# Layer 2 mixers: the last level of an inverse on one block, attention in two parts, another order at the seam

## The chip, the core and the metric

The kernel runs on one core of one Trainium2 chip. The metric is the device time of one launch in microseconds (us). Engines are named as in the profile: PE is TensorE (matmuls and transposes), DVE is VectorE, ACT is ScalarE, POOL is GpSimd, SP is SyncE, whose queue issues the DMAs. All data is float32.

## The reference, cut to what matters

The program is two layers on 1024 positions of 1024 features. Layer 2 projects its input, runs three mixers side by side (windowed attention with sinks, a state-space mixer called SSD, a gated delta rule called GDN), multiplies by an output matrix and ends with a feed-forward part. Only the mixers and what feeds them are touched.

```python
proj = h @ w_in
(a_q, a_k, a_v, s_z, s_xbc, s_dt, g_qkv, g_z, g_b, g_a) = jnp.split(proj, offs, axis=-1)
att = swa_sink_alibi(a_q, a_k, a_v, attn_sinks)          # 4 heads, scores over 3 chunks of 64
ssd = ssd_mixer(s_z, s_xbc, s_dt, ...)
gdn = gdn_mixer(g_qkv, g_z, g_b, g_a, ...)               # 4 heads
mix = jnp.concatenate([att, ssd, gdn], axis=-1) @ w_out

# in gdn_mixer, per head and chunk of 64:
strict = jnp.tril(kbeta @ k.T * decay, -1)
u, w = split(triangular_solve(I + strict, [v * beta, kbeta * exp(g)]))
v_new = u - w @ state
o = (q * exp(g)) @ state + (q @ k.T * decay) @ v_new
state = state * exp(g_last) + (k * exp(g_last - g)).T @ v_new
```

## The kernel before

**Stages.** Layer 1, then `layer2_projections` (24 units of 128 features: 14 through a convolution, 6 through a silu, 4 plain), `layer2_mixers`, the output product, and the feed-forward part, which takes the last third of the time. Each stage is a block at whose end the engines meet.

**Tiles.** `layer2_mixers` goes through 8 tiles of 128 positions (NT = 8). For GDN a tile is taken as one piece: its lower triangular matrix of 128x128 per head is inverted by doubling. A level b (2, 4, 8, 16, 32, 64) joins pairs of inverted blocks of b by b. With V the inverse so far (transposed) and VT its transpose, a level is

- `level_t(b)` on PE: the turn Y (V into VT, bank 7, copied by ACT), then T = NM_b x V for four heads into bank 5, where NM_b is the matrix times the mask of the level, made by POOL;
- a copy of T by ACT into T1 (`product(b)`), then `level_x(b)` on PE: X, the product of VT and T1, into bank 6;
- `level(b)` on DVE: V = V - X.

At level 64 the product goes into bank 7 instead and DVE corrects VT, which is what the chain reads next. T2, X2, Y2, V2 ... T64, X64, VT64 below are these steps. At level 64 only one block of a head isn't zero: 64 rows by 64 columns. Before, all of 128x128 is multiplied, copied and subtracted.

**Front and chain.** One round of the loop, `tile(n, i, t)`, works on the front of tile n (features turned, the scores of attention, SSD, the matrix of GDN) and on the chain of tile i = n - 1 (the six levels, then `wt`, `vn`, `o`, `ds`: the state's recurrence). The steps of both are written out in one order for each engine, and each engine takes its instructions in that order. The rounds: the front of tile 0 alone, seven rounds with front and chain (tiles 1 to 7 in front), and the chain of tile 7 alone. Signals are counters, one for each engine and each of front and chain (`Steps`): `done` raises it, `wait` waits for a step of the same tile, `wait_last` for that of the tile before.

**The steps named later**, with lines of the kernel before:

- PE: tr1 to tr4 and tr0 turn features into banks 1 to 4 and 0 (L2147); `ptr` turns the exponentials of attention, 8 pieces of 128x128 from `m_scores`; `yo` (m_ssd_state, m_bc); `v1t` turns VT0; `wt` (m_vt, m_kbg); `att` (m_v_prev or m_ga, with m_ptr); `vn` (m_gdn_state, m_wt and m_vbt, m_vt); `y` (m_xdt, m_sd); `o` (m_gdn_state, m_qgt and m_vn, m_qkd_chain); `ds` (m_vn, m_kd); `stn` (m_xde, m_vb). Matmuls are all recorded at L2151.
- DVE: `ysc` scales two sums of squares (L2018), V2 to V32 (L2012), VT64 (L2014), `xdt`, `xdec`, `yx` on SSD (L2088, L2090, L2100), `att` (L2104), `oss` (L2109), `og` (L2119), `y` (L2123), `yz` (L2125), `ogz` (L2130), `st2`, the new SSD state (L2134).
- ACT: two squares of Y with their sums (`yq0`, `yq1`, L1919), then `yln` and `yexp` on what ysc left, the copies of z and ga, VT2 (L1896) and T4 (L1899); four exponentials e0 to e3 (L1967), `es` (L1968), `pt`, the copy of the turned ones (L1971); the copy of `wt` (L1980).
- POOL: `nm0` to `nm5` (L1877), `kbg`, `kd`, `gzn` (L1849, waits for ogz of the tile before), `qgt`, `qkdc` and `bc` (copies, L47).

**Entry.** The projections write features to DRAM from ACT's results. The first 20 are read back for tile 0 while the last four are still being computed; these four (q, k and v of attention) are read back in `layer2_mixers` (L1818) when both stores have landed, and PE and POOL wait for `f_late`.

## Time and profile before

| | |
|---|---|
| three runs | 2499.05, 2503.95, 2503.97 us (median 2503.95) |
| profiled execution | 2499.8 us, its span 2498.0 us |
| PE, PEld, DVE, ACT, POOL busy in the span | 95%, 79%, 60%, 45%, 14% |
| granted PE clock, mean | 0.987 |
| layer-2 mixers | 1410 to 1733 us of the span |
| chain that ended last | 24% PE, nearly all in the feed-forward stage |

The page gives each engine's busy time over the whole span; the chain of waits on it covers only the end of the program, from 1848 us. The touched stage has to be read by itself, with windows and timelines.

### The profile page before, as it was taken

The numbers are of one execution on the slowest core, as the hardware profiler recorded it, in microseconds if no ns is written. First come the engines' busy times: TensorE is split into PE (matmuls) and PEld (weight loads), VectorE is DVE, ScalarE is ACT, GpSimd is POOL, SyncE is SP. The second block draws the span as 40 slices with busy tenths as digits, with TensorE's granted clock in tenths as the row PEclk, the third lists the DMA queues.
The fourth block names the chain that finished last, engine by engine and source line by source line (L and its number), as shares of the span: only waits on it lengthen the run. The fifth ranks groups of instructions, "written<-read, shape, count | busy, mean of one in ns | idle before, by whom it ended". The sixth has DMA issues, their size and how long they took to land. (4 is left out here: it accounts for less than half of the span.)

```text
span 2498.0 us, 33605 instructions
## 1 busy us (share of the span) xinstructions
PE 2369.3 (95%) x11568; PEld 1962.8 (79%) x11568; DVE 1506.1 (60%) x2096; ACT 1114.5 (45%) x1998; POOL 347.6 (14%) x361
## 2 busy tenths in 40 slices
PE   7999999999899999999999889987999999999997
PEld 6888888877778877787887778876877888888886
DVE  4657566665665546564551377775578677776556
ACT  4867677677443321242222255454333333323444
POOL 0423333333100000000000145442000000000000
PEclk9999999999999999999999899999999999999999
DMA  3111111110132264422223422211324434437764
GB/s 134 43 34 61 35 44 51 56 39 26 59 135 101 97 231 164 148 110 75 92 87 140 127 64 63 63 38 43 125 103 165 160 143 164 163 139 262 237 187 169
DMA packets 102886, 273.37 MB, mean 109 GB/s; under 512 B 9372, under 2 KB 35452, under 8 KB 98300
## 3 DMA queue, kind: packets, MB, share of 16 engines
q1 hardware_dynamic: 102780, 272.01, 31.5%
q8 instruction: 61, 1.00, 0.2%
q14 instruction: 45, 0.37, 0.1%
HBM read 196.16 MB, written 75.81 MB: 109 GB/s over the span
## 5 line engine op out<-in xcount | busy, mean ns | idle before, releaser
L52 PE MATMUL psG<-h_hi,w_hi 128*128 128x512 f32 x1056 | 262.6, 397 | 11.3 <-PEq L309 4.4
L52 PE MATMUL psG<-h_hi,w_lo 128*128 128x512 f32 x1056 | 257.8, 392 | 0.0
L52 PE MATMUL psG<-h_lo,w_hi 128*128 128x512 f32 x1056 | 257.5, 391 | 0.0
L52 PEld LDWEIGHTS psG<-h_hi,w_hi 128*128 128x128 f32 x1056 | 200.2, 192 | 55.4 <-issue 13.6
L82 DVE TENSOR_TENSOR w_lo<-w_raw,w_hi 128x1024 fp32r<-128x1024 f32 x82 | 104.8, 1280 | 223.5 <-ACT w_hi L77 223.1
L52 PEld LDWEIGHTS psG<-h_lo,w_hi 128*128 128x128 f32 x1056 | 198.6, 189 | 41.6
L52 PEld LDWEIGHTS psG<-h_hi,w_lo 128*128 128x128 f32 x1056 | 198.0, 188 | 41.3
L77 ACT CAST w_hi<-w_raw 128x1024 fp32r<-128x1024 f32 x84 | 88.0, 1048 | 146.7 <-PE psG L52 67.7
L366 POOL TENSOR_TENSOR sb_later_lo<-sb_later,sb_later_hi 128x512 fp32r<-128x512 f32 (+3 forms) x80 | 90.7, 1133 | 169.5 <-ACT sb_later_hi L395 169.5
L1831 POOL MEMSET m_k_prev<- 128x128 f32 x1 | 0.2, 204 | 770.1 <-POOLq L1517 770.1
L530 DVE SCALAR_TENSOR_TENSOR sb_sp<-psA,sb_tmp 128x128 f32<-128x128 f32 (+2 forms) x96 | 53.4, 556 | 73.5 <-ACT sb_tmp L384 72.8
L547 DVE TENSOR_TENSOR sb_w_lo<-sb_w,sb_w_hi 128x128 fp32r<-128x128 f32 (+2 forms) x96 | 64.0, 666 | 53.3 <-ACT sb_w_hi L402 52.1
L401 ACT ACTIVATE sb_w<-psA 128x128 f32<-128x128 f32 (+2 forms) x96 | 47.1, 491 | 86.6 <-PE psA L713 84.9
L363 POOL TENSOR_TENSOR sb_later<-sb_later,sb_sp 128x128 f32<-128x128 f32 (+2 forms) x64 | 70.5, 1102 | 27.5 <-DVE sb_sp L530 27.5
L1877 POOL TENSOR_TENSOR m_nm<-m_ntr,m_masks 128x512 f32<-128x512 f32 x48 | 64.5, 1373 | 68.8 <-DVE m_vt L2078 68.8
L47 POOL TENSOR_TENSOR sb_later<-sb_sp,sb_zero 128x128 f32<-128x128 f32 x56 | 42.1, 753 | 216.4 <-DVE sb_sp L534 216.4
L540 DVE TENSOR_TENSOR sb_sp_lo<-sb_sp,sb_sp_hi 128x128 fp32r<-128x128 f32 (+2 forms) x96 | 65.8, 685 | 0.0
L2674 DVE TENSOR_TENSOR h_ffn_lo<-ff_raw_up,h_ffn_hi 128x512 fp32r<-128x512 f32 x49 | 33.7, 690 | 43.9 <-ACT h_ffn_hi L2540 22.0
L2674 DVE TENSOR_TENSOR features_T<-ff_y,features_T 128x512 f32<-128x512 f32 x50 | 34.5, 690 | 39.9 <-PE ff_y L52 39.9
L2540 ACT CAST ff_a_hi<-features_T 128x512 fp32r<-128x512 f32 x40 | 24.6, 622 | 75.0 <-PE psH L52 34.6
L1620 DVE SCALAR_TENSOR_TENSOR p_acc<-p_raw,p_par,p_acc 128x1024 f32<-128x1024 f32 x42 | 54.0, 1285 | 5.5 <-DVE p_acc L1616 1.1
L2674 DVE TENSOR_TENSOR w_lo<-ff_raw_up,w_hi 128x512 fp32r<-128x512 f32 x39 | 27.0, 691 | 45.8 <-ACT w_hi L2632 45.8
(573 smaller groups left out, 5757.7 us busy)
## 6 DMA issues: line engine op xcount, KB each, us to landing
w_raw<-in_units SPq DMA_DIRECT2D x120, 512.0 KB, 4.1
w_raw<-hidden_blocks SPq DMA_DIRECT2D x77, 256.0 KB, 2.9
merge_gates<-features_T SPq DMA_DIRECT2D x12, 1024.0 KB, 7.3
merge_gates<-merge_gates SPq DMA_DIRECT2D x12, 1024.0 KB, 4.8
...
```

The source lines that it names most:

```text
L52: return pe.matmul(out, lhs, rhs, start=first, stop=last, skip_group_check=True)
L77: act.copy(self.hi[c % 2][:] if dest is None else dest, self.raw[c % 2][:]).then_inc(self.hi_done, 1)
L82: dve.tensor_tensor(self.lo[c % 2][:] if dest is None else dest, self.raw[c % 2][:], hi.bitcast(F32), ALU.subtract).then_inc(self.lo_done, 1)
L363: pool.tensor_tensor(later[:, q1:], later[:, q1:], sp_s[:, q1:], ALU.add).then_inc(later_ready, 1)
L366: pool.tensor_tensor(later_lo[(s + 1) % 2][:, q0:], later[:, q0:], later_hi[(s + 1) % 2][:, q0:].bitcast(F32), ALU.subtract).then_inc(late ...
L401: act.activation(w_t[:, first_query(s):], A[s % 3][:, first_query(s):], ACT.Exp).then_inc(exp2_done, 1)
L530: ins = dve.scalar_tensor_tensor(out[:, q0:], A[s % 3][:, q0:], 0.0, tmp[:, q0:], ALU.max, ALU.add)
L540: dve.tensor_tensor(sp_lo[s % 2][:, q0:], sp_t[s % 2][:, q0:], sp_hi[s % 2][:, q0:].bitcast(F32), ALU.subtract).then_inc(sp_lo_done, 1)
L547: dve.tensor_tensor(w_lo[s % 2][:, q0:], w_t[:, q0:], w_hi[s % 2][:, q0:].bitcast(F32), ALU.subtract).then_inc(w_lo_done, 1)
L1620: dve.scalar_tensor_tensor(acc[b][:], raw[b][:, t:t + T], par[:, bass.ds(n, 1), t], acc[b][:], ALU.mult, ALU.add).then_inc(step if t else ...
L1877: poolF.done(f"nm{m}", g.tensor_tensor(NM[:, m], NTR[:], over(MSK[:, 2 + m, :], GH), ALU.mult))
L2674: TT = lambda o, a, b, op: dve.tensor_tensor(o, a, b, op)
```

## The change

Five edits:

1. **Level 64.** T64, its copy, X64 and VT64 are cut to the block that isn't zero: T64 into partitions 64 to 127 and 64 columns per head, X64 into partitions 0 to 63 and 64 columns.
2. **Attention in two parts.** The turn of the exponentials waits for heads 0 and 1 and then for heads 2 and 3 (e1, e3) instead of for `es`. The products of attention for heads 0 and 1 stand ahead of `wt`, those of heads 2 and 3 behind it.
3. **DVE at the seam.** V2 comes first in a round, then `st2` of the tile before, then `ysc`.
4. **DVE at the end of a round.** `ogz` comes straight behind `og`, ahead of `y` and `yz`.
5. **Late features.** In the projections ACT writes the first 128 positions of each of the last four features from PSUM straight into tile 0's buffer, by one multiplication each ahead of the one it does anyway; the DMA at L1818 goes.

```diff
                             scale = 64 ** -0.5 if c < CONV + SILU + 2 else 1.0
+                            act.mul(D2.F[:, c, :], G[b][:, 0:P], scale).then_inc(D2.f_late, 1)
                             act.mul(res[b][:], G[b][:], scale).then_inc(silu_done[b], 1)
...
-                sp.dma_start(F[:, AQ0:, :], feats[AQ0:, :, 0:P].rearrange("c p t -> p c t")).then_inc(f_late, 16)
...
-                        scalG.done(f"T{b}", a.copy(T1[:].rearrange("p h t -> p (h t)"), bank(5)))
+                        if b < 64:
+                            scalG.done(f"T{b}", a.copy(T1[:].rearrange("p h t -> p (h t)"), bank(5)))
+                        else:
+                            scalG.done("T64", a.copy(T1[64:, :, 0:64], heads(PS[64:, 5, :], GH)[:, :, 0:64]))
...
-                            vectG.done("VT64", tt(flat(VT), flat(VT), bank(7), ALU.subtract))
-
+                            vectG.done("VT64", tt(VT[0:64, :, 64:], VT[0:64, :, 64:], heads(PS[0:64, 7, :], GH)[:, :, 64:], ALU.subtract))
+
+                    level(2)
                     if chain:
+                        vectF.wait(v, "st1", i)
+                        tensF.wait(v, "stn", i)
+                        vectF.done("st2", tt(ST[:], ST[:], bank(0), ALU.add))
                         scalG.wait(v, "yq1", i)
                         vectG.done("ysc", v.tensor_scalar(yss[:], yss[:], 1.0 / 256, EPS, ALU.mult, ALU.add))
-                    level(2)
...
                         for h in range(GH):
+                            if b == 64:
+                                x = mm(PS[64:, 5, h * P:h * P + 64], NM[:, LEVELS.index(b), h, 64:], V[:, h, 0:64])
+                                continue
                             x = mm(PS[:, 5, h * P:(h + 1) * P], NM[:, LEVELS.index(b), h], (V0 if b == 2 else V)[:, h])
...
-                                x = mm(PS[:, 7, h * P:(h + 1) * P], T1[:, h], vt[:, h])
+                                x = mm(PS[0:64, 7, h * P + 64:(h + 1) * P], T1[:, h, 0:64], vt[:, h, 64:])
...
-                        scalF.wait(pe, "es", n)
-                        turn(tensF, "ptr", 1, [SS[:, h, m * P:(m + 1) * P] for h in range(AH) for m in range(2)])
+                        for h in range(AH):
+                            if h % 2 == 0:
+                                scalF.wait(pe, f"e{h + 1}", n)
+                            for m in range(2):
+                                x = pe.transpose(PS[:, 1 + h // 2, (2 * (h % 2) + m) * P:(2 * (h % 2) + m + 1) * P], SS[:, h, m * P:(m + 1) * P], C["ident"][:])
+                        tensF.done("ptr", x)
...
                         turn(tensF, "v1t", 3, [VT0[:, h] for h in range(GH)])
+                        scalF.wait(pe, "pt", n)
+                        scalF.wait(pe, "ga", n)
+                        poolF.wait_last(pe, "vprev", n)
+                        attention(0)
```

`attention(first)` is the loop of before over two of the four heads. Not shown: the lines of `ogz` and `st2` at their old places, and that `f_late` is now waited for at 4 (one for each feature).

DVE at the seam from one round to the next, before (L1803 ends the loop's round; og, y, yz, ogz and st2 belong to the round that ends, ysc and V2 to the next):

```order
L2119 TENSOR_TENSOR m_og<-m_ps,m_orr 128x256 [waits m2_scalar_chain]
...
L2123 TENSOR_TENSOR m_y<-m_y,m_ps 128x512 [waits m2_vector_front]
...
L2125 TENSOR_TENSOR m_y<-m_y,m_z 128x512 [waits m2_vector_front]
...
L2130 TENSOR_TENSOR m_mix<-m_og,m_gzn 128x256 [waits m2_tensor_turned,m2_gpsimd_chain]
...
L2134 TENSOR_TENSOR m_ssd_state<-m_ssd_state,m_ps 128x512 [waits m2_tensor_front]
...
L2018 TENSOR_SCALAR m_yss<-m_yss 128x2 [waits m2_scalar_chain]
L2012 TENSOR_TENSOR m_v<-m_v,m_ps 128x512 [waits m2_scalar_front,m2_tensor_chain]
```

and after:

```order
L2125 TENSOR_TENSOR m_og<-m_ps,m_orr 128x256 [waits m2_scalar_chain]
...
L2129 TENSOR_TENSOR m_mix<-m_og,m_gzn 128x256 [waits m2_tensor_turned,m2_gpsimd_chain]
...
L2133 TENSOR_TENSOR m_y<-m_y,m_ps 128x512 [waits m2_vector_front]
...
L2135 TENSOR_TENSOR m_y<-m_y,m_z 128x512 [waits m2_vector_front]
...
L2015 TENSOR_TENSOR m_v<-m_v,m_ps 128x512 [waits m2_scalar_front,m2_tensor_chain]
L2023 TENSOR_TENSOR m_ssd_state<-m_ssd_state,m_ps 128x512 [waits m2_tensor_front,m2_vector_front]
L2025 TENSOR_SCALAR m_yss<-m_yss 128x2 [waits m2_scalar_chain]
```

ogz has moved up past y and yz, st2 has moved into the next round behind V2, and ysc (m_yss), which waits for ACT, stands behind both.

PE from the turn of the scores to wt, before (m_scores is ptr; m_v,m_nm is T64; m_vt,m_t is X64; c_ident,m_vt is v1t; m_kbg is wt):

```order
L2147 MATMUL m_ps<-c_ident,m_scores 128x128 [waits m2_scalar_front]
L2147 MATMUL m_ps<-c_ident,m_scores 128x128 x7
...
L2166 MATMUL m_ps<-c_ident,m_v 128x128 [waits m2_vector_chain]
L2166 MATMUL m_ps<-c_ident,m_v 128x128 x3
...
L2151 MATMUL m_ps<-m_v,m_nm 128x128 [waits m2_gpsimd_front]
L2151 MATMUL m_ps<-m_v,m_nm 128x128 x3
...
L2151 MATMUL m_ps<-m_vt,m_t 128x128 [waits m2_scalar_chain]
L2151 MATMUL m_ps<-m_vt,m_t 128x128 x3
...
L2147 MATMUL m_ps<-c_ident,m_vt 128x128 [waits m2_vector_front]
L2147 MATMUL m_ps<-c_ident,m_vt 128x128 x3
...
L2151 MATMUL m_ps<-m_vt,m_kbg 64x128 [waits m2_gpsimd_chain]
L2151 MATMUL m_ps<-m_vt,m_kbg 64x128 x3
```

and after:

```order
L2280 MATMUL m_ps<-c_ident,m_scores 128x128 [waits m2_scalar_front]
L2280 MATMUL m_ps<-c_ident,m_scores 128x128 x3
...
L2280 MATMUL m_ps<-c_ident,m_scores 128x128 [waits m2_scalar_front]
L2280 MATMUL m_ps<-c_ident,m_scores 128x128 x3
...
L2152 MATMUL m_ps<-m_v,m_nm 64x64 [waits m2_gpsimd_front]
L2152 MATMUL m_ps<-m_v,m_nm 64x64 x3
...
L2152 MATMUL m_ps<-m_vt,m_t 64x64 [waits m2_scalar_chain]
L2152 MATMUL m_ps<-m_vt,m_t 64x64 x3
...
L2148 MATMUL m_ps<-c_ident,m_vt 128x128 [waits m2_vector_front]
...
L2152 MATMUL m_ps<-m_v_prev,m_ptr 128x64 [waits m2_gpsimd_front]
...
L2152 MATMUL m_ps<-m_vt,m_kbg 64x128 [waits m2_gpsimd_chain]
L2152 MATMUL m_ps<-m_vt,m_kbg 64x128 x3
```

The turn waits twice, T64 and X64 have 64 partitions by 64 columns per head, and attention's first products (m_v_prev and m_ga, four in all) stand ahead of wt.

## Rows read from the trace of the kernel before

**Rows 1.** Windows: us, busy PE, PEld, DVE, ACT, POOL; PEclk, DMA, GB/s.

```profile
1415.00:1430.00 15.00, 11.78 (x61) 10.27 (x62) 11.31 (x15) 6.47 (x17) 3.24 (x4) 0.57 0.41 105
1547.63:1586.41 38.78, 35.06 (x280) 31.69 (x280) 27.29 (x47) 19.30 (x46) 17.32 (x20) 0.96 0.21 61
1661.34:1698.81 37.47, 33.44 (x281) 30.15 (x280) 27.23 (x47) 19.30 (x46) 17.28 (x20) 1.00 0.00 0
```

**Rows 2.** Timeline, PE, entry: start, us, engine line op, [idle before <-releaser].

```profile
1415.18 0.99 PE L2147 MATMUL m_ps<-c_ident,m_feat 128*128 128x128 f32 x7 [1.78 <-DMA m_feat<-features]
```

**Rows 3.** Timeline, ACT, entry.

```profile
1408.13 1.02 ACT L1572 ACTIVATE p_res<-psG 128x1024 f32<-128x1024 f32 x1 [9.85 <-PE psG L52]
```

**Rows 4.** Timeline, PE, back half of tile 4.

```profile
1572.82 1.09 PE L2147 MATMUL m_ps<-c_ident,m_scores 128*128 128x128 f32 x8 [0.64 <-ACT m_es L1968]
1573.75 0.60 PE L2166 MATMUL m_ps<-c_ident,m_v 128*128 128x128 f32 x4
1574.18 1.06 PE L2151 MATMUL m_ps<-m_v,m_nm 128*128 128x128 f32 x8
...
1576.06 1.16 PE L2151 MATMUL m_ps<-m_vt,m_t 128*128 128x128 f32 x8
1577.06 0.60 PE L2147 MATMUL m_ps<-c_ident,m_vt 128*128 128x128 f32 x4
1578.08 0.66 PE L2151 MATMUL m_ps<-m_vt,m_kbg 128*64 128x128 f32 x8 [0.42 <-DVE m_vt L2014]
...
1584.17 0.45 PE L2151 MATMUL m_ps<-m_vn,m_kd 128*64 128x64 f32 x8
```

**Rows 5.** Timeline, ACT, back half of tile 4.

```profile
1571.10 0.50 ACT L1967 ACTIVATE m_scores<-m_scores,m_ngm 128x256 f32<-128x256 f32 x1
...
1574.02 1.01 ACT L1971 COPY m_ptr<-m_ps 128x1024 f32<-128x1024 f32 x1 [1.25 <-PE m_ps L2147]
...
1575.41 0.60 ACT L1899 COPY m_t<-m_ps 128x512 f32<-128x512 f32 x1
...
1578.78 0.39 ACT L1980 ACTIVATE m_wt<-m_ps 128x256 f32<-128x256 f32 x1 [0.42 <-PE m_ps L2151]
```

**Rows 6.** Timeline, DVE, back half of tile 4.

```profile
1572.53 0.68 DVE L2012 TENSOR_TENSOR m_v<-m_v,m_ps 128x512 f32<-128x512 f32 x1
...
1577.26 0.69 DVE L2014 TENSOR_TENSOR m_vt<-m_vt,m_ps 128x512 f32<-128x512 f32 x1 [2.72 <-PE m_ps L2151]
...
1584.69 0.42 DVE L2109 TENSOR_REDUCE m_oss<-m_sqo 128x4 f32<-128x256 f32 x1 [1.45 <-ACT m_sqo L1984]
```

**Rows 7.** Timeline, PE, head of tile 5.

```profile
1588.40 1.15 PE L2151 MATMUL m_ps<-m_t,m_vt 128*128 128x128 f32 x8
...
1592.26 0.66 PE L2166 MATMUL m_ps<-c_ident,m_v 128*128 128x128 f32 x4 [1.94 <-DVE m_v L2012]
...
1594.55 1.16 PE L2151 MATMUL m_ps<-m_t,m_vt 128*128 128x128 f32 x8 [0.31 <-ACT m_t L1899]
```

**Rows 8.** Timeline, DVE, head of tile 5.

```profile
1587.83 1.04 DVE L2125 TENSOR_TENSOR m_y<-m_y,m_z 128x512 f32<-128x512 f32 x1
...
1589.13 0.67 DVE L2134 TENSOR_TENSOR m_ssd_state<-m_ssd_state,m_ps 128x512 f32<-128x512 f32 x1
1590.63 0.98 DVE L2018 TENSOR_SCALAR m_yss<-m_yss 128x2 f32<-128x2 f32 x1 [0.82 <-ACT m_sq L1919]
```

**Rows 9.** Timeline, POOL, head of tile 5.

```profile
1589.29 0.73 POOL L1849 TENSOR_TENSOR m_gzn<-m_ga,m_par_rows 128x256 f32<-128x256 f32 x1 [0.36 <-DVE m_mix L2130]
...
1590.55 1.04 POOL L47 TENSOR_TENSOR m_qkd_chain<-m_qkd,m_zero 128x512 f32<-128x512 f32 x1
...
1591.72 1.04 POOL L47 TENSOR_TENSOR m_bc<-m_feat,m_zero 128x512 f32<-128x512 f32 x1
```

**Rows 10.** Timeline, ACT, head of tile 5.

```profile
1593.91 0.59 ACT L1899 COPY m_t<-m_ps 128x512 f32<-128x512 f32 x1 [0.31 <-PE m_ps L2151]
```

**Rows 11.** Timeline, PE, last tile alone.

```profile
1703.15 0.66 PE L2166 MATMUL m_ps<-c_ident,m_v 128*128 128x128 f32 x4 [1.45 <-DVE m_v L2012]
```

More of the change, by code:

```diff
@@ L1793, in layer2_mixers @@
                                            "yo yx att st1 y yz st2")
-        vectG = Steps(sem("vector_chain"), "ysc V2 ym0 ym1 V4 V8 V16 V32 VT64 oss osc s0 s1 s2 s3 og ogz")
+        vectG = Steps(sem("vector_chain"), "V2 ysc ym0 ym1 V4 V8 V16 V32 VT64 oss osc s0 s1 s2 s3 og ogz")
         poolF = Steps(sem("gpsimd_front"), "par keep0 keep1 xd kprev nm0 nm1 nm2 vbt nm3 nm4 nm5 vprev")
@@ L1862, in tile @@
                         poolF.wait_last(g, "kprev", n)
-                        g.wait_ge(f_late, 16)
+                        g.wait_ge(f_late, PLAIN)
                         poolF.done("keep1", copy(g, AQK[:], F[:, AQ0:AQ0 + 3, :], zero))
@@ L2119, in tile @@
                         vectG.done("og", tt(heads(OG[:], GH), heads(PS[:, 6, 0:256], GH), per(orr[:], GH, 64), ALU.mult))
+                        vectG.wait(v, "og", i)
+                        poolG.wait(v, "gzn", i)
+                        tensH.wait_last(v, "mtrg", i)
+                        vectG.done("ogz", tt(M[:, 768:1024], OG[:], GZN[:], ALU.mult))
                     if front:
@@ L2125, in tile @@
                         vectF.done("yz", tt(Y[:], Y[:], Z[:], ALU.mult))
-                    if chain:
-                        vectG.wait(v, "og", i)
-                        poolG.wait(v, "gzn", i)
-                        tensH.wait_last(v, "mtrg", i)
-                        vectG.done("ogz", tt(M[:, 768:1024], OG[:], GZN[:], ALU.mult))
-                    if front:
-                        vectF.wait(v, "st1", n)
-                        tensF.wait(v, "stn", n)
-                        vectF.done("st2", tt(ST[:], ST[:], bank(0), ALU.add))
                 tiles(v, tile)
@@ L2286, in tile @@
                     if front:
-                        scalF.wait(pe, "pt", n)
-                        scalF.wait(pe, "ga", n)
-                        poolF.wait_last(pe, "vprev", n)
-                        for h in range(AH):
-                            kv = 64 * (h // 2)
-                            mm(PS[:, 1, 64 * h:64 * h + 64], PTR[:, 2 * h], VP[:, kv:kv + 64], True, False)
-                            x = mm(PS[:, 1, 64 * h:64 * h + 64], PTR[:, 2 * h + 1], GA[:, 256 + kv:320 + kv], False, True)
-                        tensF.done("att", x)
+                        tensF.done("att", attention(2))
                     if chain:
```

8 lines of the change are left out of this document (7 added, 1 removed).

## The prediction

> **What bounds the kernel now.** I read the windows view first, cut at the tiles of the layer-2 mixers, then the timelines of PE, ACT, DVE and POOL through one steady tile (tile 4 ends and tile 5 begins in it), then the entry and the tail. Only the mixer stage is touched: from 1410 to 1733 us of a span of 2498 us. The rest must keep its time, and the feed-forward stage behind it starts when the mixers end, so each us off this stage is a us off the whole.
>
> In the windows view the reader is to see that a steady tile takes 37.47 us and that PE is busy for 33.44 us of it, DVE for 27.23, ACT for 19.30, POOL for 17.28 [rows 1]. PE has the longest queue, but 4 us of idle time are left in it. The timelines show where: 1.94 us before Y2 (the turn after level 2), 0.31 before X4, 0.64 before the turn of the scores, 0.42 before wt [rows 4, 7]. So a tile goes at PE's pace except at four handovers, and both fewer PE instructions and shorter handovers count. There are seven periods from one T2 to the next, then a tail in which the last tile is alone.
>
> **Part 1, late features (once).** Before, PE waits 1.78 us for the DMA of the last four features [rows 2]. After, ACT writes them from PSUM, so the DMA and this wait go; nothing else holds PE there, as the three other turns are already done. Of the four new multiplications three lie beside PE's long products. The fourth stands ahead of the last big one, at 1408.13, for which the block's end waits [rows 3]. No row shows ACT on 128x128 from PSUM: between nothing and the 0.39 us of a 128x256 [rows 5]. I take 0.25. The DVE work behind this turn (the whole front of tile 0) shifts with it. Saved: 1.78 - 0.25 = 1.5 us; bounds 1.4 to 1.8, and less if another start-up step was just as late, which I put at 0.
>
> **Part 2, the back half of a tile (seven times).** Step by step, from the end of X32:
> - Turn of the scores. PE waits till 1572.82 for all exponentials. Exponential 1 runs at 1571.10 [rows 5], so it is done before X32 ends at 1572.18 - (0.64 of idle before 1572.82). Four of eight turns now go there; the other four wait for e3, which ends just before es, at about 1572.7, and take half of 0.93 (1572.82 to 1573.75). They end at 1573.2. Then Y32 wants V32, which ends at 1572.53 + 0.68 = 1573.21 [rows 6]. Y32 starts at about 1573.26 instead of 1573.75: 0.49 saved. With a later e3 it is 0.3; it can't be more, V32 is next.
> - T64 becomes 64 weight columns by 64 moving columns, four times. The trace has this form: ds, four matmuls in 0.45 us, where T64 takes 1.06 [rows 4]; less the overlap of about 0.1 us at their ends, 0.5 us saved. Bounds: nothing, if a fixed cost per matmul and not its size sets the pace, and 0.6. I take the row of the same form.
> - X64 waits for ACT's copy of T64 as well as for PE. ACT: the copy of the turned scores starts as their second half ends, 0.63 earlier than 1574.02 (1573.39), so the T64 copy starts at 1574.78 instead of 1575.41, and on 64x256 takes at most the 0.39 us of the 128x256 [rows 5]. It ends at 1575.16; PE is free at 1576.06 - 0.49 - 0.5 = 1575.07. X64 starts at 1575.2 instead of 1576.06, 0.86 saved, with ACT the later by 0.1.
> - X64 has the form of ds too: 0.38 us till the next instruction instead of 1.00 (1576.06 to 1577.06). 0.62 saved.
> - The turn behind it (v1t) to wt took 1.02 us (1577.06 to 1578.08), of which four turns are 0.47 and the rest is the wait for VT64. Now half of the attention stands in between, and VT64 is ready: before, it started 1.20 after X64 [rows 4, 6]; now at 1575.2 + 1.20 - 0.62 = 1575.8, and on 64x256 it takes at most the 0.42 of oss, so it ends at 1576.2, 1.75 earlier. The wait goes: 0.55 saved. What is late next: the copy of wt on ACT, hidden behind the other half of the attention.
> In sum 0.49 + 0.5 - 0.1 + 0.62 + 0.55 = 2.0 us, after which PE's queue is full up to the next T2. Its cover on DVE: DVE idled 1.45 us before oss [rows 6]; oss moves up by 2.0, the work from VT64 on by 1.75, so 1.2 us of cover is left. Seven times 2.0 = 14.0 us.
>
> **Part 3, the seam (seven times).** Before, V2 on DVE stood behind ysc, which waits for ACT's squares and ends at 1591.61; X2 was done at 1589.55 [rows 7, 8]. Now V2 starts at 1589.6 and Y2 follows the turns that end at 1592.26 - 1.94 = 1590.32. So Y2 and T4 come 1.9 us earlier. But X4 does not, as ACT must first do ysc's followers (ln, exp), the copies of z and ga and VT2, and only then T4. What X4 gains is (a) the 0.31 us that ACT waited for T4 [rows 10], and (b) whatever ysc gains. ysc stands behind st2 now and can start at 1589.6 + 0.6 + 0.6 = 1590.8, 0.2 later than before. Its end, though, was set elsewhere: it took 0.98 us for two numbers and ended 0.02 us after POOL's qkdc (1590.55 + 1.04) [rows 8, 9]. qkdc comes 0.36 us earlier, as ogz goes ahead of y and POOL no longer waits for it at gzn [rows 9]. So (b) is 0.36. X4: 0.67 us earlier, seven times 4.7 us. Bounds: -0.5 (below) to 1.0 us a tile, if ysc found DVE free of POOL. ogz ahead of y makes yz end 0.34 later, at 1589.2; the squares that read it start at 1589.7 and V2 at 1589.6, so it costs nothing. st2 after V2 ends before PE's next use of the state and of bank 0.
>
> By the Trainium skill (SBUF — State Buffer, "Who interferes with whom") DVE and GpSimd share a pair of ports, and a DVE instruction with two inputs in SBUF, or a tensor_scalar in a two-port mode, is held for a whole GpSimd instruction. The trace agrees at ysc and at yz (1.04 us, where st2 on the same shape, with one input in PSUM, takes 0.67) [rows 8]. By that rule ogz and yz, moved under kbg and kd, may be held by up to 0.6 us each, which the slack of 0.5 us nearly hides.
>
> **Part 4, the tail (once).** V2 no longer stands behind ysc: of 1.45 us of idle time before Y2 [rows 11] 0.5 goes. T64's and X64's forms and VT64 give 0.6 + 0.7 + 0.3, with nothing beside them. 2.1 us.
>
> **Sum.** 1.5 + 14.0 + 4.7 + 2.1 = 22.3 us. The profiled execution took 2499.8 us, the three runs 2499.05, 2503.97, 2503.95: the same program is found at two levels 4 to 5 us apart, so the sum is taken from between, 2501.9. That gives 2479.6; from 2499.8 it would be 2477.5, from 2503.95 2481.7. One term is left out: in tile 4 the granted clock was 0.96 and the tile took 38.78 us, 1.3 more than its sisters [rows 1]; such a dip may go or another come.
>
> **Rivals.**
> - Held ports (0.18). ysc now starts 0.2 us later. If it misses the end of qkdc it ends with bc, 1592.76 - 0.36 = 1592.4 [rows 9], 0.8 later than before; less 0.31 that is a loss of 0.5 a tile instead of a gain of 0.67, 8 us in seven. For it: both moved edges are within 0.4 us. Against: the same instruction got through at qkdc's end in the tile shown. The same mechanism could use up the 1.2 us of cover before oss (yx and xdec have two inputs in SBUF; a POOL instruction on 128x512 is 1.04 us, and two of them are more than 1.2). 2488.
> - Narrow products no cheaper (0.08). T64 and X64 keep 0.9 and 1.0 us because writing or reading a half of the partitions costs the same. Then 1.1 us a tile and in the tail goes: 22.3 - 8.9 = 13.4, 2488.5. Against it: ds, the same form.
> - PE slower (0.04), the one that ends on the other side. The granted clock is at half for most of tile 0 (0.57 from 1415 to 1430 us) [rows 1], where PE had idled and waited; the change leaves PE idle in one piece of 1.5 us before X4, with narrower work around it. A dip costs 1.3 us [rows 1], so 17 dips in seven tiles, two or three in each, eat the gain; three in each make 2507. Against: the four idle pieces of a tile fall from 3.3 us to about 1.9 in sum, and before had one dip in seven periods.
> - More than forecast (0.10): tile 0 goes at full clock, or ysc runs free: 2472 to 2474.
> - That PE waits as before because the order is not what it says is excluded by the instruction order.
>
> **Numbers.** Forecast 0.60, with its own range 2475 to 2485. Over all cases: 2472 to 2491. A change within 0.2% (5 us, about what can be told from none) needs nearly all of part 2 to fail: 0.02. Slower by more than that 0.03, faster 0.95.
>
> **What would show it.** The period from T2 to T2 at 34.8 us instead of 37.47; T64 and X64 at about 0.45 us each; no idle time before wt; before Y2 less than 0.1 us of idle time and 1.4 us before X4, ended by ACT; ysc ending with qkdc; oss still waiting for ACT; no DMA wait at 1413 us. Wrong would be: an idle PE before y or o (DVE late), ysc ending with bc, a granted clock under 0.97 from tile 1 on.

## The result, and the profile after

The kernel after takes 2487.93 us (median of 6 runs, 2484.43 to 2491.8), the kernel before 2503.81 us beside it (6 runs, 2499.05 to 2505.5). The ratio is 0.9940, interval 0.9928 to 0.9952: 16 us faster, where 22.3 were forecast. The time lies 8 us above the likeliest number, 2479.6; 2 of them come from the kernel before, which took 2503.8 and not the 2501.9 that the sum started from. The profiled execution took 2485.86 us, its span 2484.1 us.

| us, from the starts of PE's rows | before | after | gained | forecast |
|---|---|---|---|---|
| first turn of the mixers to T2 of tile 1's round | 25.06 | 22.32 | 2.7 | 1.5 |
| seven periods from T2 to T2 | 263.14 | 251.41 | 11.7 | 18.7 |
| last T2 to the first output product | 36.62 | 35.45 | 1.2 | 2.1 |
| the mixers | 324.82 | 309.18 | 15.6 | 22.3 |

So the shortfall lies in the periods. (The first row starts behind the new multiplications, whose 0.18 us is not in it.) Window of a steady tile after (columns as in [rows 1]):

```profile
1579.42:1615.17 35.75, 32.98 (x281) 29.41 (x280) 29.03 (x47) 19.09 (x47) 17.88 (x20) 1.00 0.23 66
```

A tile takes 35.74 us, not 34.8. PE has only 0.5 us less to do than in [rows 1], and DVE, whose VT64 now takes 0.41 us and not 0.69, is busy for 1.8 us more. That is the first trace of the cause.

PE, back half of a tile, against [rows 4]:

```profile
1566.45 1.36 PE L2280 MATMUL m_ps<-c_ident,m_scores 128*128 128x128 f32 x8
1567.69 0.66 PE L2167 MATMUL m_ps<-c_ident,m_v 128*128 128x128 f32 x4
1568.28 0.68 PE L2152 MATMUL m_ps<-m_v,m_nm 128*64 128x64 f32 x8
1568.89 1.13 PE L2152 MATMUL m_ps<-m_ssd_state,m_bc 128*128 128x256 f32 x4
1569.95 0.68 PE L2152 MATMUL m_ps<-m_vt,m_t 128*64 128x64 f32 x8
1570.56 0.66 PE L2148 MATMUL m_ps<-c_ident,m_vt 128*128 128x128 f32 x4
...
1571.98 0.66 PE L2152 MATMUL m_ps<-m_vt,m_kbg 128*64 128x128 f32 x8
```

Its weight loads (PEld) at three places where the width of the weights changes (128*64 stands for 64 weight columns):

```profile
1568.28 0.54 PEld L2152 LDWEIGHTS m_ps<-m_v,m_nm 128*64 128x64 f32 x8 [0.17 <-issue]
...
1569.95 0.54 PEld L2152 LDWEIGHTS m_ps<-m_vt,m_t 128*64 128x64 f32 x8 [0.33 <-ACT m_t L1902]
...
1572.57 0.30 PEld L2152 LDWEIGHTS m_ps<-m_v_prev,m_ptr 128*128 128x128 f32 x2 [0.17 <-issue]
```

T64 and X64 take 0.68 us, not 0.45; there is no idle time before wt. Before T64, and behind wt, PEld stands still for 0.17 us with nothing to wait for; behind T64 and behind X64, where the width changes as well, it is 0.07 us. Before X64 it waits 0.33 us for ACT's copy of T64.

PE at the head of the next round, against [rows 7]:

```profile
1584.02 0.66 PE L2167 MATMUL m_ps<-c_ident,m_v 128*128 128x128 f32 x4 [0.70 <-DVE m_v L2015]
...
1587.27 1.16 PE L2152 MATMUL m_ps<-m_t,m_vt 128*128 128x128 f32 x8 [1.26 <-ACT m_t L1900]
```

DVE from the back half to the head, against [rows 6, 8]:

```profile
1572.20 1.22 DVE L2094 TENSOR_TENSOR m_xdt<-m_xs,m_par 128x512 f32<-128x512 f32 x1
...
1575.17 1.08 DVE L2106 TENSOR_TENSOR m_y<-m_y,m_xd 128x512 f32<-128x512 f32 x1
...
1576.52 1.42 DVE L2111 TENSOR_TENSOR m_ssd_state<-m_ssd_state,m_par 128x512 f32<-128x512 f32 x1
1577.86 0.40 DVE L2115 TENSOR_REDUCE m_oss<-m_sqo 128x4 f32<-128x256 f32 x1
1578.30 0.79 DVE L2117 TENSOR_SCALAR m_oss<-m_oss 128x4 f32<-128x4 f32 x1
...
1580.86 0.65 DVE L2129 TENSOR_TENSOR m_mix<-m_og,m_gzn 128x256 f32<-128x256 f32 x1 [0.19 <-DVE m_og L2125]
1581.43 0.67 DVE L2133 TENSOR_TENSOR m_y<-m_y,m_ps 128x512 f32<-128x512 f32 x1
1582.14 1.23 DVE L2135 TENSOR_TENSOR m_y<-m_y,m_z 128x512 f32<-128x512 f32 x1
1583.29 0.67 DVE L2015 TENSOR_TENSOR m_v<-m_v,m_ps 128x512 f32<-128x512 f32 x1
...
1584.49 0.38 DVE L2025 TENSOR_SCALAR m_yss<-m_yss 128x2 f32<-128x2 f32 x1
```

DVE has no idle time before oss any more: xdt, yx and the decay of the SSD state (L2111) take 1.08 to 1.42 us beside POOL, where they took 0.69, 0.69 and 0.80. ogz takes 0.65 us and starts 0.19 after og, whose result it reads; yz ends 3.95 us behind T2 (before: 2.46), and V2 starts straight behind it.

One short instruction matters for what follows: `osc`, which scales the four sums of oss (L2117). In every period of all fourteen kernels og starts 1.15 to 1.16 us behind its end, and it ends itself 0.02 to 0.03 us behind an nm of POOL. Before, it took 0.48 us; first DVE, then POOL, before and after:

```profile
1585.15 0.48 DVE L2111 TENSOR_SCALAR m_oss<-m_oss 128x4 f32<-128x4 f32 x1
```

```profile
1582.66 4.17 POOL L1877 TENSOR_TENSOR m_nm<-m_ntr,m_masks 128x512 f32<-128x512 f32 x3
```

```profile
1575.67 4.63 POOL L1877 TENSOR_TENSOR m_nm<-m_ntr,m_masks 128x512 f32<-128x512 f32 x3
```

The three nm start 3.75 us ahead of T2 in both. After, they take 0.46 us more, all of it in the second one (1.71 us, before 1.27), beside the decay, which now stands under it. osc ends 0.03 us behind that second nm after, 0.02 before; so it ends 0.45 later against T2, and og with it. In the last tile, where POOL makes no nm, osc takes 0.17 us in every kernel.

ACT and POOL beside it, against [rows 10] and [rows 9]:

```profile
1583.40 0.42 ACT L1922 ACTIVATE m_sq<-m_y 128x256 f32<-128x256 f32 x1 [0.59 <-DVE m_y L2135]
```

```profile
1582.09 0.73 POOL L1849 TENSOR_TENSOR m_gzn<-m_ga,m_par_rows 128x256 f32<-128x256 f32 x1
1582.78 1.06 POOL L47 TENSOR_TENSOR m_qgt<-m_qt,m_zero 128x256 f32<-128x256 f32 x1
1583.80 1.03 POOL L47 TENSOR_TENSOR m_qkd_chain<-m_qkd,m_zero 128x512 f32<-128x512 f32 x1
```

The squares now wait 0.59 us for yz. ysc ends 0.04 us after qkdc (before: 0.02). POOL no longer waits at gzn, as forecast, but qgt takes 1.06 us where it took 0.61, beside yz, and ends 0.47 us behind yz's end.

The entry, PE and ACT, and the tail, against [rows 2, 3, 11]:

```profile
1412.91 3.80 PE L2148 MATMUL m_ps<-c_ident,m_feat 128*128 128x128 f32 x19 [2.68 <-DVEq L1726]
```

```profile
1410.26 0.28 ACT L1572 ACTIVATE m_feat<-psG 128x128 f32<-128x128 f32 x1 [9.69 <-PE psG L52]
```

```profile
1691.22 0.66 PE L2167 MATMUL m_ps<-c_ident,m_v 128*128 128x128 f32 x4 [1.69 <-DVE m_v L2015]
```

The DMA wait is gone. The multiplication delays the last big one by 0.18 us (1410.26 to 1410.44).

### The profile page after: what moved, and what is told of

It reads as the page before. It is cut to its first block and busy times, and to the rows that moved or that the text cites. A ratio compares the mean times of both kernels' runs of the same rounds, so it can differ in the third digit from the quotient of the medians.

```text
span 2484.1 us, 33608 instructions
## 1 busy us (share of the span) xinstructions
PE 2360.2 (95%) x11568; PEld 1953.0 (79%) x11568; DVE 1517.1 (61%) x2096; ACT 1112.5 (45%) x2002; POOL 351.4 (14%) x361
## 5 line engine op out<-in xcount | busy, mean ns | idle before, releaser
L2152 PE MATMUL m_ps<-m_t,m_vt 128*128 128x128 f32 x320 | 46.2, 288 | 14.7 <-ACT m_t L1900 14.3
```

## Two distances

A period splits at X4, where PE waits for ACT. In every kernel below I took from a steady tile of its one profiled execution: the head (T2 to X4), the rest (X4 to the next T2), and, counted from T2, the end of ysc on DVE and of the POOL instruction that ends next to it.

| kernel | head | rest | period | ysc | POOL |
|---|---|---|---|---|---|
| before | 8.14 | 29.32 | 37.46 | 4.22-5.20 | qkdc 5.18 |
| seam alone | 7.60 | 29.32 | 36.92 | 4.47-5.20 | qkdc 5.17 |
| back half alone | 7.59 | 27.91 | 35.50 | 4.22-4.66 | qgt 4.63 |
| after, ogz behind yz | 7.07 | 27.90 | 34.97 | 4.47-4.66 | qgt 4.64 |
| after | 7.85 | 27.90 | 35.75 | 5.07-5.45 | qkdc 5.41 |
| after, SD early | 7.63 | 27.90 | 35.53 | 4.85-5.22 | qkdc 5.20 |
| after, attention whole | 7.47 | 28.46 | 35.93 | 4.69-5.07 | qkdc 5.04 |
| after, old seam | 9.66 | 27.90 | 37.56 | 4.93-5.45 | qkdc 5.43 |

With V2 first, X4 follows 2.40 us behind ysc's end, so the head is a matter of when ysc ends. That has two parts: when it can start, and whether a POOL instruction holds it. ysc ends within 0.04 us of the end of a POOL instruction each time. Where that is qkdc, it takes 0.37 to 0.98 us. Where it has started ahead of qkdc it ends with qgt, after 0.19 us with V2 first (the shortest that any run shows is 0.17) and 0.44 without. The kernel before has both: in the tile from 1510.90 on, ysc starts 0.16 us ahead of qkdc and takes 0.22 us, the head is 7.46 and the period 36.78; in the other tiles from 1473 us on, but the last, it ends with qkdc.

A steady tile repeats within 0.05 us in most of these kernels, so differences of period are read from it; the ratios below alone don't tell all of them apart (SD early and the kernel after, for one, have intervals that overlap).

## Experiments

Numbers behind the name: median, ratio to the kernel before, interval of the ratio. Edits are cut to the lines that move; lines left out are marked by three dots.

### Parts taken out of the kernel after

**Level 64 in full** (2489.9 us, 0.995, 0.9933 to 0.9967).

```diff
-                            if b == 64:
-                                x = mm(PS[64:, 5, h * P:h * P + 64], NM[:, LEVELS.index(b), h, 64:], V[:, h, 0:64])
-                                continue
...
-                                x = mm(PS[0:64, 7, h * P + 64:(h + 1) * P], T1[:, h, 0:64], vt[:, h, 64:])
+                                x = mm(PS[:, 7, h * P:(h + 1) * P], T1[:, h], vt[:, h])
```

(and the copy and VT64 on all of 128x512)

> The changed kernel with level 64 on all of 128x128 again (T64, its copy, X64, VT64). The prediction's step (the form of ds, 0.095 us a matmul): narrow forms save 0.5 + 0.62 us on PE, so the period is 36.7 to 36.8 us. Theory N (a group of narrow stationary blocks pays about 0.17 us in front and behind, when the array's shape changes and no weights are loaded ahead): from Y32 to yo 1.33 instead of 1.20 us, from X64 to the turn behind it 1.00 instead of 0.61, and in all a period of 36.2 to 36.35 us.

Period 36.18: head 7.91, rest 28.27. The cut gives 0.37 us in the rest, 0.44 in the period, where the prediction had 1.1 (T64 and X64). From start to start, T64 takes 0.61 instead of 0.89 and X64 0.61 instead of 0.99, but the steps ahead of them, Y32 and yo, take 0.59 instead of 0.49 and 1.06 instead of 0.92. From Y32 to X64 it is 2.26 instead of 2.30: what T64 gives is lost again, as X64 waits for ACT's copy of T64 in both (PEld 0.33 us, here 0.28). So nearly all of the 0.37 is X64's 0.38. The head is 0.07 longer here: osc takes 0.99 us, with POOL's second nm ending later still.

**SD early on DVE** (2485.89 us, 0.9926, 0.9909 to 0.9943).

```diff
                         vectF.done("vt1", tt(VT0[:], VT0[:], over(C["ident"][:], GH), ALU.add))
...
+                        for g in range(2):
+                            vectF.done(f"sd{g}", tt(SD[:, 4 * g:4 * g + 4], DEC[:, 4 * g:4 * g + 4],
+                                                    over(PS[:, 0, P * g:P * g + P], 4), ALU.mult))
```

(the same lines go from their place behind VT64)

> The changed kernel with one more move on DVE: the two products sd0 and sd1 stand ahead of VT64 (where DVE idled 1.69 us) instead of behind it. Period from T2 to T2 in the changed kernel: 35.73 us. Theory P (held ports use up the cover): DVE runs without a pause from VT64 to V2, held by POOL at xdt, yx, st1, osc, ogz and yz, so yz ends late and the squares and X4 with it; with 1.2 us of DVE work taken from in front, oss waits for ACT again, yz ends 0.3 to 0.5 us earlier after T2 and the period is 35.3 to 35.5 us, about 2.5 us less in all. Rival S (st2 ahead of ysc is what makes ysc late, not yz): DVE's earlier end changes nothing in the head, 35.7 us.

Period 35.53. oss waits again (1.20 us), yz ends 0.2 earlier. That is less than the expected 0.25 to 0.45, and it isn't the cover itself that is worth it: osc ends 0.21 earlier against T2, 0.02 behind POOL's second nm, which ends 0.20 earlier. With level 64 in full oss waits too (0.94 us), and og comes 0.89 us behind T2, later than after (0.82). So it is the stretch in which DVE and POOL hold each other that costs, and not the missing wait before oss.

**ogz behind yz again** (2483.29 us, 0.9915, 0.9898 to 0.9931).

```diff
-                        vectG.done("ogz", tt(M[:, 768:1024], OG[:], GZN[:], ALU.mult))
...
                         vectF.done("yz", tt(Y[:], Y[:], Z[:], ALU.mult))
+                        vectG.done("ogz", tt(M[:, 768:1024], OG[:], GZN[:], ALU.mult))
```

> The changed kernel with ogz back behind yz. Theory P: ogz in front of y costs 0.19 us of wait, 0.65 us of its own (0.42 free of POOL) and pushes yz, which is on the path; back at its place yz ends 0.6 us earlier, the squares start right behind vb, and the period falls from 35.73 to about 35.4 us, although POOL's gzn waits for ogz again. The step of the prediction (POOL's 0.36 us at gzn is what ysc needs): the period grows to 36.1 us, with ysc ending with qkdc.

Period 34.97: 0.77 us gained, all in the head. yz ends 2.92 us behind T2 instead of 3.95. DVE, POOL and PE in that kernel:

```profile
1583.36 0.19 DVE L2025 TENSOR_SCALAR m_yss<-m_yss 128x2 f32<-128x2 f32 x1
```

```profile
1582.22 0.73 POOL L1849 TENSOR_TENSOR m_gzn<-m_ga,m_par_rows 128x256 f32<-128x256 f32 x1 [0.36 <-DVE m_mix L2136]
1582.91 0.62 POOL L47 TENSOR_TENSOR m_qgt<-m_qt,m_zero 128x256 f32<-128x256 f32 x1
1583.48 1.04 POOL L47 TENSOR_TENSOR m_qkd_chain<-m_qkd,m_zero 128x512 f32<-128x512 f32 x1
```

```profile
1585.96 1.16 PE L2153 MATMUL m_ps<-m_t,m_vt 128*128 128x128 f32 x8 [1.07 <-ACT m_t L1900]
```

ysc ends at 1583.55, 0.02 after qgt and in front of qkdc's hold, though POOL waits its 0.36 us at gzn as before. Of the 0.78 us that ysc ends earlier, 0.60 are its earlier start (4.47 behind T2 instead of 5.07) and 0.18 that it takes 0.19 us and not 0.37. The later POOL is the better one: ysc gets through ahead of qkdc. Theory P had the direction but less than half of the size (0.33).

**Old seam** (V2 behind ysc, st2 at the end; 2502.49 us, 0.9995, 0.9985 to 1.0004).

```diff
-                    level(2)
                     if chain:
...
-                        vectF.done("st2", tt(ST[:], ST[:], bank(0), ALU.add))
...
                         vectG.done("ysc", v.tensor_scalar(yss[:], yss[:], 1.0 / 256, EPS, ALU.mult, ALU.add))
+                    level(2)
...
                         vectF.done("yz", tt(Y[:], Y[:], Z[:], ALU.mult))
...
+                        vectF.done("st2", tt(ST[:], ST[:], bank(0), ALU.add))
```

> The changed kernel with DVE's old order at the seam: st2 at the end of the round, then ysc, then V2. As predicted for this edit, X4 is bound by ACT and Y2 coming early gives 0.31 us a period: 36.0 to 36.1 us instead of 35.73, PE idle about 2 us before Y2. Theory P adds that DVE is late already, so V2 behind st2 and ysc comes at T2 + 5.8 us and T4 gets later than ACT's copies: up to 36.3 us. If the seam's order is worth the two us of wait that it removed, 37.0 us or more.

Period 37.56: all of the periods' gain is gone. PE, and the window of that tile:

```profile
1593.77 1.11 PE L2168 MATMUL m_ps<-c_ident,m_v 128*128 128x128 f32 x4 [2.19 <-DVE m_v L2015]
1594.68 1.91 PE L2153 MATMUL m_ps<-m_v,m_nm 128*128 128x128 f32 x8
```

```profile
1587.68:1625.24 37.56, 34.52 (x280) 30.93 (x279) 28.80 (x47) 19.30 (x47) 17.88 (x20) 0.95 0.22 63
```

Y2 and T4 take 1.11 and 1.91 us where they took 0.66 and 1.06: behind 2.19 us of idle time PE runs at the lower of its two clock levels, and the granted clock of the tile is 0.95. The periods from the second on are alike (37.55 to 37.59), so it happens in each of them. Idle time before Y2 is not all that decides: before, six of the seven periods have 1.94 to 2.12 us of it (one has 1.26), and only one of those shows a granted clock of 0.96. In the kernel before, X4 starts 2.35 us behind V2's end (8.14 - 5.79), here 3.62 (9.66 - 6.04): 1.27 us of the 1.81 lost are the clock, 0.54 the later V2.

**Attention whole** (2490.14 us, 0.9951, 0.9934 to 0.9967).

```diff
-                        for h in range(AH):
-                            if h % 2 == 0:
-                                scalF.wait(pe, f"e{h + 1}", n)
...
+                        scalF.wait(pe, "es", n)
+                        turn(tensF, "ptr", 1, [SS[:, h, m * P:(m + 1) * P] for h in range(AH) for m in range(2)])
...
-                        attention(0)
```

(its two heads stand behind wt again)

> The changed kernel with attention in one piece again (turn of the scores waits for es, wt ahead of all of the attention). The prediction's step (turn 0.49, wait before wt 0.55, less what the early VT64 gives anyway): 0.5 to 0.6 us a tile back, period 36.2 to 36.4. A rival: PE is no longer the bound of a tile but DVE and ACT, so PE's 0.5 us hide in the idle time before Y2 and X4 and the period stays at 35.7 to 35.9.

Period 35.93. The rest is 0.56 us longer, as the prediction's step says, but the head is 0.38 shorter: osc takes 0.55 us and not 0.79 and ends 0.38 earlier against T2, so og and everything behind it do, ysc's end too. The period falls between the two expectations, nearer to that of the rival, but not for its reason. In the kernel after, splitting attention is worth 0.19 us.

**Full weights, 64 moving columns** (2491.95 us, 0.996, 0.9946 to 0.9974).

```diff
-                                x = mm(PS[64:, 5, h * P:h * P + 64], NM[:, LEVELS.index(b), h, 64:], V[:, h, 0:64])
+                                x = mm(PS[:, 5, h * P:h * P + 64], NM[:, LEVELS.index(b), h], V[:, h, 0:64])
```

(X64 in the same way)

> The changed kernel with T64 and X64 as products of 128 weight columns by 64 moving columns (the unneeded half of the partitions is written and not read). If what narrow weights cost is a fixed 0.17 us each time PE goes over to 64 columns and back, T64 and X64 lose 2 to 3 such pieces, 0.3 to 0.5 us, and the period is 35.3 to 35.5. If the cost lies in the number of products and not in the width of the weights: 35.7 to 35.8, as the changed kernel. If narrow weights load faster and that is what counts: 35.9 to 36.1.

```profile
1567.55 1.00 PE L2152 MATMUL m_ps<-m_v,m_nm 128*128 128x64 f32 x8
...
1569.31 1.03 PE L2152 MATMUL m_ps<-m_vt,m_t 128*128 128x64 f32 x8
```

Period 35.9, rest 28.10. Halving the moving columns alone (with the narrower copy) gives 0.17 us of the 0.37, 0.05 before X64 and 0.13 in it. Halving the weights gives the other 0.20: 0.26 in X64, less 0.05 behind it. My guess that narrow weights cost more at the changes of width than they bring is wrong.

### Parts put alone into the kernel before

**Seam alone** (2498.56 us, 0.9989, 0.998 to 0.9999).

```diff
+                    level(2)
                     if chain:
...
+                        vectF.done("st2", tt(ST[:], ST[:], bank(0), ALU.add))
...
                         vectG.done("ysc", v.tensor_scalar(yss[:], yss[:], 1.0 / 256, EPS, ALU.mult, ALU.add))
-                    level(2)
...
```

(st2 goes from its place behind ogz)

> The kernel before with nothing changed but the seam: V2 first in a round, then st2, then ysc; ogz stays behind yz. Head bound by DVE (my theory now): V2 no longer waits for the squares, so PE's 1.94 us of idle time before Y2 goes, and X4 comes as early as with ogz behind yz in the changed kernel, 7.1 us behind T2 instead of 8.14; with the old way from X4 to the next T2 (29.3) the period is 36.4, the time 8 us under the kernel before. The prediction's step: the turn is free, but X4 gains only the 0.31 us that ACT waited, period 37.1 to 37.2, 2 to 2.5 us. Seam alone carries all of the change: period 35.7.

Period 36.92: 0.54 us, between the prediction's 0.31 and my 1.07. PE's idle time before Y2 is gone and stands before X4 (1.61 us). ysc ends at 5.20, with qkdc, in the same place as before: V2 first doesn't move the handover to ACT, and only the wait for T4 and some 0.2 us beside it (VT2's copy no longer waits for Y2) are gained.

**Back half alone** (level 64, attention, late features; 2490.77 us, 0.9947, 0.9931 to 0.9964). Against the kernel after, the edits of the old seam and of ogz together.

> The kernel before with the back half alone (level 64 cut, attention in two parts) and the late features; seam and ogz in the old order. The prediction's part 2, 2.0 us a tile by itself: period 35.5. My theory now, that the head hangs from DVE's end of y z (the squares read it, ysc waits for the squares, V2 for ysc) and that DVE had only 1.2 us of cover before oss, of which POOL's holding takes more: about what is measured with ogz ahead of y (37.56) less the 0.77 that ogz was found to cost, 36.8. Nothing of the back half shows at all: 37.4 to 37.6.

Period 35.50: the prediction's number, and my theory of lost cover falls. But the number doesn't come for the prediction's reasons. The rest gained 1.42 us, not 2.0. The other 0.55 us are the head's: DVE and POOL stand 0.45 later against T2, qkdc starts at 4.59 instead of 4.14, and ysc, which starts at 4.22 as before, is held by qgt and not by qkdc. It ends 0.54 earlier:

```profile
1586.46 0.44 DVE L2021 TENSOR_SCALAR m_yss<-m_yss 128x2 f32<-128x2 f32 x1 [0.37 <-ACT m_sq L1922]
```

```profile
1586.26 0.61 POOL L47 TENSOR_TENSOR m_qgt<-m_qt,m_zero 128x256 f32<-128x256 f32 x1
1586.83 1.04 POOL L47 TENSOR_TENSOR m_qkd_chain<-m_qkd,m_zero 128x512 f32<-128x512 f32 x1
```

The two parts add up: 1.96 and 0.54 make 2.50, and with both, ogz left in place, it is 2.49 (37.46 to 34.97).

**Level 64 alone** (2498.71 us, 0.9983, 0.9972 to 0.9993). The first edit of the change in the kernel before, nothing else.

> The kernel before with level 64 cut, nothing else. By the 0.45 us that the cut is worth in the changed kernel: period 37.0. By the prediction (0.5 + 0.62 on PE, and VT64 early enough for wt): 36.0 to 36.3. If in the old order DVE's work behind VT64 takes it back, as the seam does with the whole back half: 37.2 to 37.5.

Periods 36.84, 37.90, 35.95, 37.77, 35.92, 36.69, 37.89: none of the theories had that. The rest is 28.46 where the clock holds, 0.86 less than before (0.37 of it between the turn of VT0 and vn, where wt no longer waits for VT64). Two things jump. One is the clock: the three periods of 37.8 to 37.9 us show a granted clock of 0.95, the others 1.00. The other is the head, from the second period on 7.5 us where ysc is ahead of qkdc and 8.2 to 8.3 where it is not and the clock holds. Two tiles, DVE and then POOL in each:

```profile
1553.70 1.06 DVE L2021 TENSOR_SCALAR m_yss<-m_yss 128x2 f32<-128x2 f32 x1 [0.76 <-ACT m_sq L1922]
```

```profile
1553.70 1.04 POOL L47 TENSOR_TENSOR m_qkd_chain<-m_qkd,m_zero 128x512 f32<-128x512 f32 x1
```

```profile
1591.47 0.17 DVE L2021 TENSOR_SCALAR m_yss<-m_yss 128x2 f32<-128x2 f32 x1 [0.73 <-ACT m_sq L1922]
```

```profile
1591.48 1.06 POOL L47 TENSOR_TENSOR m_qkd_chain<-m_qkd,m_zero 128x512 f32<-128x512 f32 x1
```

In one tile both start at the same time and the two numbers take 1.06 us; in the other ysc is 0.01 us ahead and takes 0.17. A hundredth of a microsecond decides over 0.89. (The periods of these two tiles differ by 1.85: 0.83 of it in the head, the rest behind X4, where the first has the lower clock.)

### Versions that might be faster

**ogz back, VT2 and T4 first on ACT** (2475.02 us, 0.9894, 0.9878 to 0.9911).

```diff
+                    if chain:
+                        product(4)
                     if front:
...
                         scalF.done("z", a.copy(Z[:], bank(3)))
...
                         scalF.done("ga", a.copy(GA[:], PS[:, 4, 0:384]))
-                    if chain:
-                        product(4)
```

> The changed kernel with ogz behind yz again, and on ACT the copies of VT2 and of T4 straight behind yexp, ahead of those of z and ga. If X4 is the path of the head and ACT's two copies (0.75 to 0.87 us together) stand in it: X4 at 6.2 to 6.3 us behind T2 instead of 7.07, period 34.1 to 34.3 instead of 34.97. If what follows from z and ga on DVE and POOL is as late as X4: period 34.9 to 35.2, nothing gained. If PE's queue fills up before that: 34.5.

Period 34.21, head 6.31, as the first of the three expectations had it; the fastest kernel of all, by the two ratios 0.46%, 11.5 us, under the kernel after. Window, ACT and PE:

```profile
1572.78:1606.99 34.21, 32.97 (x280) 29.41 (x279) 28.95 (x47) 19.09 (x47) 18.50 (x20) 1.00 0.24 69
```

```profile
1578.45 0.58 ACT L1900 COPY m_t<-m_ps 128x512 f32<-128x512 f32 x1
```

```profile
1579.09 1.16 PE L2153 MATMUL m_ps<-m_t,m_vt 128*128 128x128 f32 x8 [0.31 <-ACT m_t L1900]
```

**And SD early** (2483.82 us, 0.9922, 0.9905 to 0.9938). The second experiment's edit in addition.

> The changed kernel with ogz behind yz, VT2 and T4 copied first on ACT, and SD's two products ahead of VT64 on DVE. If V2 hangs from X2 now and no longer from DVE's queue: period 34.1 to 34.3, as without the third edit (34.21). If DVE's queue still sets the head: the same 0.2 us as in the changed kernel, 34.0.

Period 34.91, 0.7 us worse, outside both. In the kernel after this edit gained 0.2. Here it moves ogz 0.19 earlier, so POOL is earlier, so qkdc starts before ysc:

```profile
1584.31 0.99 DVE L2025 TENSOR_SCALAR m_yss<-m_yss 128x2 f32<-128x2 f32 x1
```

```profile
1584.23 1.04 POOL L47 TENSOR_TENSOR m_qkd_chain<-m_qkd,m_zero 128x512 f32<-128x512 f32 x1
```

**Or ysc ahead of st2** (2483.97 us, 0.9919, 0.9897 to 0.9941).

```diff
                     if chain:
...
+                        vectG.done("ysc", v.tensor_scalar(yss[:], yss[:], 1.0 / 256, EPS, ALU.mult, ALU.add))
...
                         vectF.done("st2", tt(ST[:], ST[:], bank(0), ALU.add))
...
-                        vectG.done("ysc", v.tensor_scalar(yss[:], yss[:], 1.0 / 256, EPS, ALU.mult, ALU.add))
```

> As with ogz behind yz and VT2 and T4 copied first, and ysc ahead of st2: V2, ysc, st2. ysc can start when the squares end, 4.2 us behind T2, instead of 4.47 behind st2. If the way to X4 goes through ysc: X4 0.27 us earlier, period 33.95. If ysc is held by POOL's copies there: up to 0.6 us later than now, period 34.5 to 34.8. If X4 is set by PE: 34.2.

Period 34.94, 0.7 us worse. X4 stays at 6.31: ysc starts 0.25 earlier, is held by qgt and ends at 4.66 as before. But st2 and what follows are 0.6 to 0.7 us later on DVE, the scaling of q's and k's sums (m_ss) then takes 0.94 us and not 0.37, ending 0.02 behind POOL's bc, and PE waits at the turn of Y's features behind X4:

```profile
1583.30 0.94 DVE L2031 SCALAR_TENSOR_TENSOR m_ss<-m_ss,m_par_rows 128x8 f32<-128x8 f32 x1
```

```profile
1585.74 0.87 PE L2149 MATMUL m_ps<-c_ident,m_mix 128*128 128x128 f32 x6 [0.63 <-DVE m_mix L2038]
```

## Why the prediction was right, and where it failed

The time lay in the range over all cases, 2472 to 2491, and the direction was right; it missed the range of the forecast itself, 2475 to 2485, and the likeliest number was 8 us too low. 2488 is the number of two rivals, held ports and narrow products, and both came true in part: about 4 us of the shortfall are the back half's, 3 the head's. Neither came as priced: ysc ended with qkdc and not with bc, and T64 and X64 did get cheaper. By its steps:

- **Part 1, 1.5 us: right in kind, priced too low.** 1.78 of DMA wait go, 0.18 of multiplication come. The stage shows 2.7 behind the first turn. The kernel with attention whole has this edit without the second one, and its T2 comes 22.53 us behind the first turn, where it was 25.06: 2.53, so 2.35 with the multiplication. Up to the end of VT0 on DVE 1.68 us are gained (17.33 behind the first turn instead of 19.01). Behind it PE's clock is better (yo takes 1.28 us instead of 1.79), which the prediction named among its rivals and left out of the sum; and with attention in parts the turn of the scores no longer waits 0.50 us for es.
- **Part 2, 2.0 us a tile: the sum came out (1.96 alone), two terms didn't.** The turn of the scores gave 0.49, as forecast. T64 with its wait for ACT was to bring X64 0.4 closer and brought it 0.05: from Y32 to X64 it is 2.26 us, before 2.31, forecast 1.94 (1573.26 to 1575.2). ACT sets it, as forecast, but later: the copy of T64 starts 1.75 us behind Y32 and not 1.52, and the narrow X64 starts 0.14 behind the copy's end, the full one 0.05. X64 itself was to give 0.62 and gave 0.39. wt and the attention gave 0.49, forecast 0.55. Together 1.42; the 0.55 that made the sum whole came from the head and was luck. So two terms are mis-sized: ACT's way to the copy of T64, and the row of ds, "the same form". The products themselves are alike (columns: ns, least, median and most):

```profile
L2152 PE MATMUL m_ps<-m_v,m_nm x8: 221/222/271, 1568.3 to 1568.7; 128*64 128x64 f32 x8
```

```profile
L2152 PE MATMUL m_ps<-m_vn,m_kd x8: 221/223/271, 1577.2 to 1577.4; 128*64 128x64 f32 x8
```

but those of T64 start (0.68 - 0.22) / 7 = 0.07 us apart and those of ds (0.45 - 0.22) / 7 = 0.03. One difference in the code: ds writes its heads to partitions 0 to 63 and 64 to 127 in turn, T64 all to 64 to 127 and X64 all to 0 to 63. The single starts in the trace bear on it: in ds the products start in pairs 0.01 us apart, and so they do in wt, which also writes in turn, while T64 and X64 have no such pair, every product starting about 0.06 behind the last. That writing in turn is what lets products overlap fits these four steps, but no kernel was run with T64 in turns; it stays open.
- **"1.2 us of cover is left": wrong.** Nothing was left: xdt, yx and the decay of the SSD state (L2111) grew by 0.53, 0.39 and 0.62 us, beside POOL's nm and vbt, which they now stand under. The rival "held ports" named this. But the wait that went at oss is not what made og late: oss starts only 0.16 later against T2. og's 0.45 is osc's, which ends with POOL's second nm, and that nm grew by 0.44 beside the decay. The prediction has no term for osc. No kernel was run to move osc or nm alone; it rests on the two ending together in every period of the fourteen kernels, and on osc's 0.17 us where there is no nm.
- **Part 3, (a) 0.31: measured 0.54.** Right mechanism, slightly small.
- **Part 3, (b) 0.36 and "ogz ahead of y costs nothing": this is the step that failed.** With (b) in the sum the edit was to gain 0.36; it cost 0.77 us a tile, as the kernel without it shows. yz was to end 0.34 later, at 2.8 us behind T2, under the squares' start; it ended at 3.95: og 0.45 late with osc, 0.19 of waiting for og's own result, 0.65 for ogz, 0.19 more for yz. The squares came 0.7 later than before, ysc started 0.60 later than with ogz behind yz, and it fell under qkdc, which had come 0.21 earlier just because gzn no longer waited. og's 0.45 alone did no harm: with ogz behind yz it is there too. From +0.36 to -0.77 is 1.13 us a tile, 7.9 us in seven.
- **Part 4, 2.1: measured 1.2.** Idle time before Y2 is 1.69 us, not 0.95: ogz stands ahead of y there as well, and the head is 6.91 us where it was 6.56. The other 1.5 of the 1.6 came.

Account of the seven periods: forecast 18.7, measured 11.7. The rest of a tile lacks 0.58, the head gained 0.29 where 0.67 was forecast; 0.96 a tile is 6.7 us. The single edits give 0.54 for V2 first and 0.55 for the back half, less the 0.77 of ogz: 0.32, which is the head's 0.29 to within 0.03.

The rivals: "held ports" had the place and part of the mechanism: the cover went, but ysc did not end with bc, it ended with qkdc. It priced the head 1.17 us a tile short of the forecast and 0.38 was measured, so that its 2488 was met is luck. "Narrow products no cheaper" was more than half right: of 1.1 us for T64 and X64 0.44 came. "PE slower" didn't happen here (granted 1.00 in each of the seven periods) and did with the old seam and ogz ahead of y, in every period from the second on; with the old seam and ogz behind yz (back half alone) its steady periods don't have it, PE's idle time before Y2 being 1.40 us there. Of the signs named ahead, right were: no idle time before wt, no DMA wait, about 1.4 us before X4 (1.26), ysc ending with qkdc. Wrong were T64 at 0.45, less than 0.1 us before Y2 (0.70) and oss waiting for ACT.

The traces show ysc at 1.06 and 0.17 us in two tiles of one kernel, with 0.01 us between them in when it starts against qkdc. It takes 0.99 where qkdc starts 0.08 ahead of it, and 0.19 where qkdc starts 0.12 behind. By the Trainium skill (SBUF — State Buffer, "Who interferes with whom") "issue order, not op shape, decides who blocks", and the other engine is blocked for a whole instruction; the trace agrees. The prediction used the rule on single instructions and left it out of the sum. Between steps of equal width, with nothing to wait for, PEld starts the next weights 0.03 to 0.08 us ahead of the end of the last; where the width changes it starts them 0.07 to 0.17 behind it. By the Trainium skill (TensorEngine Tiling (Array Packing), "Key Properties") a change of the tiling mode drains the engine; the trace agrees. It doesn't explain why T64 is slower than ds, which has wide neighbours too (0.07 on both sides).
